# Expert outputs weighted by their gates and added onto x in DRAM by the scatter itself; the first weight chunk loaded in halves

## What is computed

```python
x = x + mix @ w_out                      # "x2" below
xn2 = rmsnorm(x, n2)
# hier_moe: each token goes to 2 of 64 experts, with a gate for each
hdn = silu(xblk @ w1[e]) * (xblk @ w3[e])        # 1024 -> 256
yb = hdn @ w2[e]                                 # 256 -> 1024
y = segment_sum(yb * g_buf[:, None], tok_buf)    # weighted by the gate, summed by token
x = x + y
y_prompt, y_sample = rmsnorm(x, final_norm_g)
```

## Time and profile before

| | us |
|---|---|
| median of 3 runs (lowest, highest) | 1863.19 (1863.05, 1865.97) |
| the profiled execution: its time | 1865.4 |
| the profiled execution: its span | 1863.5 |
| PE busy | 1763.6 (95%) |
| DVE / ACT / POOL busy | 585.1 / 449.3 / 240.2 |

### The profile page before, as it was taken

How to read it: one execution, slowest core, us unless ns; L and a number is a source line. 1 busy time by engine, 2 the same in 40 slices (tenths; PEclk the granted TensorE clock), 3 DMA queues, 4 the chain that set the end, 5 groups by cost and what they waited for, 6 DMA issues and landing times.

```text
span 1863.5 us, 27679 instructions
## 1 busy us (share of the span) xinstructions
PE 1763.6 (95%) x11544; PEld 1477.6 (79%) x11544; DVE 585.1 (31%) x1076; ACT 449.3 (24%) x802; POOL 240.2 (13%) x297
## 2 busy tenths in 40 slices
PE   8999999999999999999999999999899888878885
PEld 8999999999888888899999998887555545544542
DVE  5000102432233323255215337655233111111115
ACT  6221225632222222231222104212111111111113
POOL 0003210000001001000000000000332222222221
PEclk9999999999999999999999999999999999999998
DMA  4222223244435535267616435244799999999997
GB/s 156 94 94 95 70 85 125 95 153 140 125 119 181 165 114 177 99 216 262 226 41 227 140 94 196 92 160 177 318 423 424 425 424 424 424 424 424 424 377 293
DMA packets 159478, 406.34 MB, mean 218 GB/s; under 512 B 20341, under 2 KB 102133, under 8 KB 134778
## 3 DMA queue, kind: packets, MB, share of 16 engines
q1 hardware_dynamic: 137402, 344.22, 49.5%
q0 software_dynamic: 21952, 60.34, 8.3%
HBM read 340.62 MB, written 79.60 MB: 225 GB/s over the span
## 4 chain that ended last, share of the span: by engine, by line
PE 88%; issue 5%; DMA 2%; DVE 2%; ACT 1%; DVEq 0%; SPq 0%; POOLq 0%; POOL 0%; ACTq 0%
PE ps L2006 16%; PE ps L2008 16%; PE ps L2007 16%; PE ps L2311 12%; PE ps L2204 7%; PE ps L2333 6%; PE ps L2298 2%; PE ps L2312 1%; PE ps L2322 1%; PE ps L2095 1%; PE ps L2105 1%; PE ps L2106 1%; PE ps L2019 1%; DMA SG<-feat 1%; PE ps L2372 1%
## 5 line engine op out<-in xcount | busy, mean ns | idle before, releaser
L2006 PE MATMUL ps<-XH,WH 128*128 128x384 f32 (+1 forms) x1152 | 383.1, 333 | 0.0
L2008 PE MATMUL ps<-XH,WL 128*128 128x384 f32 (+1 forms) x1152 | 377.4, 328 | 0.0
L2007 PE MATMUL ps<-XL,WH 128*128 128x384 f32 (+1 forms) x1152 | 377.3, 328 | 0.0
L2311 PE MATMUL ps<-E,yt 128*64 128x256 f32 x1024 | 251.9, 403 | 56.9 <-issue 55.9
L2312 PE MATMUL ps<-E,yt 128*64 128x256 f32 x1024 | 253.0, 404 | 0.0
L2311 PEld LDWEIGHTS ps<-E,yt 128*64 128x64 f32 x1024 | 143.3, 145 | 120.0 <-issue 64.3
L2006 PEld LDWEIGHTS ps<-XH,WH 128*128 128x128 f32 x1152 | 216.4, 188 | 17.0 <-issue 15.1
L2007 PEld LDWEIGHTS ps<-XL,WH 128*128 128x128 f32 x1152 | 216.6, 188 | 0.0
L2008 PEld LDWEIGHTS ps<-XH,WL 128*128 128x128 f32 x1152 | 216.4, 188 | 0.0
L2006 PE MATMUL ps<-WH,XH 128*128 128x256 f32 (+2 forms) x648 | 185.0, 285 | 4.7 <-DVE XL L1447 4.7
L1453 DVE TENSOR_TENSOR WL<-RAW,WH 128x2048 fp32r<-128x2048 f32 (+1 forms) x34 | 78.1, 2298 | 348.1 <-ACT WH L1153 347.9
(11 more groups left out here) (346 smaller groups left out, 2372.4 us busy)
## 6 DMA issues: line engine op xcount, KB each, us to landing
E<-in_exp_w_dram SPq DMA_DIRECT2D x192, 1024.0 KB, 27.7
RAW<-in_w_in_dram SPq DMA_DIRECT2D x29, 1024.0 KB, 7.8
feat<-OF POOLq DMA_DIRECT2D x20, 1088.0 KB, 8.1
SG<-feat SPq DMA_DIRECT2D x24, 544.0 KB, 4.7
tokd<-OT POOLq DMA_DIRECT2D x10, 1024.0 KB, 7.5
cbuf<-feat SPq DMA_DIRECT2D x16, 544.0 KB, 5.4
X<-in_x_prompt_dram SPq DMA_DIRECT2D x16, 512.0 KB, 3.6
VR<-tokd SPq DMA_DIRECT2D x32, 256.0 KB, 2.9
```

What stands on the lines that cost most here:

```text
L2006: pe.matmul(out, hi, mhi, start=start, stop=False)
L2007: pe.matmul(out, hi, mlo, start=False, stop=False)
L2008: return pe.matmul(out, lo, mhi, start=False, stop=stop)
L2311: pe.matmul(ps[0:BR, 2 + b, 0:DE], XT[b][:, turned(k), :], E1[s][:, 1, k, :], start=(k == 0), stop=(k == KD - 1))
```

## The change

1. **The scatter adds.** While the out projection runs, SP also stores each tile of x2 to DRAM (`keep_x2` into `x2d`, 4.5 MB in all). In the experts, ACT's copy from PSUM multiplies each row by its gate (`scale=gw[:, n]`), and POOL's scatter adds the rows onto `x2d` at the rows that were gathered (`tidx`; `yidx` and `ytok` are gone). Two scatters may not be under way at once, since a token stands in two experts, so each scatter waits until the one before it has landed.
2. **Gates earlier.** The gates must be known by slot before the first output leaves PSUM. `gate_differences`, the exponentials and `gate_weights` move ahead of the experts, 18 one-hot matrices are made by DVE after `x_copy` of expert 0, 18 matmuls on PE (`gate_slots`) sum them behind `h_t` of expert 1, and a copy makes `gw`. ACT's first `y_out` waits for it.
3. **Tail.** SP loads the sums, one row a token (0.5 MB a tile), back into `X2`. ACT squares, DVE scales, SP stores. The gate products on DVE and PE and the scaling on ACT and POOL are gone. The root's table is loaded by ACT ahead of the first tile.
4. **First weight chunk in halves.** Chunk 0 comes as two DMAs of half the rows. ACT and DVE split tile 0 of x first, then each half, and PE starts with the first half.

```diff
             def keep_x2(n):
+                sp.wait_ge(x2_ready, n + 1)
+                sp.dma_start(x2d...[n * P:n * P + rows, :], X2[0:rows, n, :]).then_inc(x2_st[0], 16)
...
-                pool.indirect_dma_start(out=ytok[:, :], out_offset=bass.IndirectOffsetOnAxis(ap=column, axis=0),
+                pool.indirect_dma_start(out=x2d[:, :], out_offset=bass.IndirectOffsetOnAxis(ap=column, axis=0),
                                         in_=YS[b][:], in_offset=None,
-                                        bounds_check=4 * NTOK - 1, oob_is_err=False).then_inc(y_st[b], 16)
+                                        bounds_check=2 * NTOK - 1, oob_is_err=False, compute_op=ALU.add).then_inc(y_st[b], 16)
...
             def scatter(st):
                 n, b = st.n, st.b
                 if n == 0:
-                    pool.wait_ge(r_ix, 2)
+                    pool.wait_ge(x2_st[0], x2_st[1] + 16 * NT)
                 pool.wait_ge(y_ready, n + 1)
-                scatter_by(yidx[:, n:n + 1], b)
+                if st.after(1):
+                    pool.wait_ge(y_st[1 - b], 16 * ((n + 1) // 2))
+                scatter_by(tidx[:, n:n + 1], b)
...
             def y_out(st):
                 if st.after(2):
                     act.wait_ge(y_st[b], st.u * 16)
-                act.activation(YS[b][:], ps[:, 5 + b, :], ACT.Copy).then_inc(y_ready, 1)
+                if st.static and n == 0:
+                    act.wait_ge(r_ix, 2)
+                weight = gw[:, n:n + 1] if st.static else gwx[:]
+                act.activation(YS[b][:], ps[:, 5 + b, :], ACT.Copy, scale=weight).then_inc(y_ready, 1)
...
             def load_c(n):
-                sp.dma_start(FY[n][0:rows], ytok.rearrange("(k n h) c -> n k (h c)", k=2, h=2)[n * P:n * P + rows]).then_inc(cy_in[n][0], 16)
+                sp.dma_start(X2[0:rows_of(n), n, :], rows_of_x2(n)).then_inc(cy_in[n][0], 16)
```

More of the change, by code:

```diff
@@ L461, in overflow @@
                 eng.wait_ge(s_over, 10)
[L463 to L467, removed]
+        GATES_AT = 1
         T_COL = [C_V + CW * i for i in range(4)] + [C_R + CW * i for i in range(4)] + [C_VV, C_VV + CW]
@@ L1102, in _ @@
             experts(expert)
+            for b in range(2):
+                pool.wait_ge(y_st[b], 16 * (NE // 2))
             def again(j):
@@ L1113, in again @@
                 wait_alone(pool, y_ready, st.n + 1)
-                scatter_by(yix[:, 0:1], 0)
+                scatter_by(gix[:, 0:1], 0)
                 wait_alone(pool, y_st[0], (j + (1 + NE // 2)) * 16)
             overflow(pool, blocks_over(pool), again)
[L1118 to L1124, removed]
             barrier(pool, 1)
@@ L1808, in index_columns, with gate_differences @@
                 dve.drain()
-                dve.scalar_tensor_tensor(out=tidx[:, c], in0=u, scalar=hv[:], in1=t, op0=ALU.add, op1=ALU.add)
+                dve.tensor_scalar(tidx[:, c], u, hv[:], None, ALU.add)
+            def gate_differences():
+                dve.tensor_tensor(gva[:], lgt[:, :, 0:GROUPS], gtop[:, :, 0:1].to_broadcast([P, NT, GROUPS]), ALU.subtract)
+                dve.tensor_tensor(gd[:], etop[:, :, 1:2], etop[:, :, 0:1], ALU.subtract)
+                dve.drain().then_inc(r_df, 1)
@@ new lines, in gate_weights @@
+            def gate_weights():
+                dve.wait_ge(r_ex, 1)
+                dve.tensor_reduce(gsm[:], gex[:], AX.X, ALU.add)
+                dve.tensor_scalar(gr[:], gd[:], 1.0, None, ALU.add)
+                dve.drain()
+                dve.tensor_tensor(gr[:], gr[:], gsm[:], ALU.mult)
+                dve.drain()
+                dve.reciprocal(gsm[:], gr[:])
+                dve.drain()
+                dve.tensor_copy(gates[:, :, 0:1], gsm[:])
+                dve.tensor_tensor(gates[:, :, 1:2], gsm[:], gd[:], ALU.mult)
+                dve.drain()
+                dve.memset(gates[NDEC:P, NFULL, :], 0.0)
+                dve.drain()
+                dve.scalar_tensor_tensor(out=gow[:], in0=rk[:], scalar=float(BR), in1=gates[:].rearrange("p t k -> p k t"), op0=ALU.is_lt, op1=ALU.mult)
+                dve.drain()
@@ new lines, in gate_one_hot, with gate_one_hots @@
+            def gate_one_hot(i):
+                return AGn[:, i, :] if i < 2 * KD else AGs[:, i - 2 * KD, :]
+            def gate_one_hots():
+                dve.wait_ge(n2_ready, NT + 1)
+                dve.wait_ge(n2_st[0], 16 * (NT // 2 + 1))
+                for i in range(2 * NT):
+                    dve.tensor_scalar(gate_one_hot(i), slf[:].rearrange("p a r -> p (a r)"), row[:, i % 2, i // 2:i // 2 + 1], gow[:, i % 2, i // 2:i // 2 + 1],
+                                      ALU.is_equal, ALU.mult)
+                dve.drain().then_inc(r_ab, 1)
@@ L1897, in over_count @@
                 dve.drain().then_inc(r_ov, 1)
-            def gate_diagonals(n):
-                rows = rows_of(n)
-                i = WEIGHED.index(n)
-                for k in range(2):
-                    dve.tensor_scalar(GD[0:rows, i, k, 0:rows], ident[0:rows, 0:rows], gates[0:rows, n, k:k + 1], None, ALU.mult)
             def x_copy(st):
@@ L2285, in over_slots, with gate_slots @@
             def over_slots(j):
-                pe.wait_ge(r_ab, NT + j + 1)
+                pe.wait_ge(r_ab, NT + 1 + j + 1)
                 for i in range(3 * j, 3 * j + 3):
-                    last = pe.matmul(ps[:, 7, 0:NOVF], A2[:, i % 6, :], B[:, i % 6, :], start=(i == 0), stop=(i == 2 * NT - 1))
+                    last = pe.matmul(ps[:, 7, 0:2 * NOVF], A2[:, i % 6, :], B[:, i % 6, :, :].rearrange("p a n -> p (a n)"), start=(i == 0), stop=(i == 2 * NT - 1))
+                last.then_inc(r_tb, 1)
+            def gate_slots():
+                pe.wait_ge(r_ab, NT + 1)
+                for i in range(2 * NT):
+                    one_hot = AGn[:, i, :] if i < 2 * KD else AGs[:, i - 2 * KD, :]
+                    last = pe.matmul(ps[:, 7, 384:384 + NE], one_hot, oh[:, i % 2, i // 2, :], start=(i == 0), stop=(i == 2 * NT - 1))
                 last.then_inc(r_tb, 1)
```

236 lines of the change are left out of this document (102 added, 134 removed).

## The result

The changed kernel takes 1932.1 us in the median of four runs (1928.0 to 1935.2), the kernel before 1864.0 beside it: a ratio of 1.0363 with a 95% interval of 1.035 to 1.0376. The profiled execution took 1929.5 us, with a span of 1927.7.

A forecast was written before the change was run, and what follows sets the result against it. The expert stage was taken as DMA-bound, 8.08 us an expert; the change would bring 8.45 us cycles. The last landing moves +38.2, the tail -16.0, so 1863.2 + 22.2 gives 1885 us, range 1845 to 1912.

The forecast's parts named there:

- the scatter's chain: Expert stage: each scatter issued only after the last landed; landing 7.6 plus 0.80 makes 8.40 us a cycle.
- the dear add: Rival, expert stage: split packets or successive read and write, landings 8.4 and more, cycle 9.2, median 1927 us; chance 0.18.
- Start: Kernel start: with the first weight chunk in halves, PE's first product comes 2.4 us earlier, at about 13.6.
- Storing x2, gates: Before the experts: last store costs 0.3 us, one-hots fit, gate matmuls take 2.5 us; first scatter at about 1337.0.
- The add's time on the engines: Expert stage: the destination is read too, twice the DMA engine time, 0.33 us more for each expert.
- The landing: Expert stage: an adding scatter lands 7.6 us after issue under load, where a plain one takes 6.8.
- The two are almost equal.: Expert stage: DMA's 8.41 and the chained scatters' 8.40 us nearly coincide, so 8.45 us a cycle was taken.
- The queue runs empty at times ... which pulls the cycle back.: Expert stage: with waits longer than DMA's 8.4 us, the queue sometimes empties and scatters land in 2.34 us, shortening the cycle.
- the prediction's own conversion from profile to median: Whole kernel: the profile's own time lies 1.9 us above its span and 2.2 us above the runs' median.
- Tail: After the last landing: loads and stores of 8.9 MB take 21.0 us of DMA, 23.7 in all, gaining 16.0.
- Neither limit binds: Rival, expert stage: the add costs engines nothing and lands within 7.3 us, cycle 8.08 to 8.12, 1846 us; chance 0.25.
- second price: First sixteen experts: tied to landings they lose their 6.90 us pace, so the stage costs nearly 64 full cycles.

The follow-up runs named there:

- rows4k: Changed kernel with the adding scatter writing whole 4 KB token rows, half as many descriptors, wait kept: 1915.4 us.
- plain_wait: Changed kernel with a plain scatter instead of the adding one, the wait for the landing before kept: 1852.6 us.
- groups: Changed kernel with experts in the order 0, 8, 16, ..., adding scatter kept, wait for the previous landing dropped: 1880.6 us.
- no_w2: Changed kernel, adding scatter and wait kept, with 59 of 64 loads of the third expert matrix left out: 1840.8 us.
- tail_no_norm: Changed kernel without the tail's final normalisation, each tile stored as soon as its load has landed: 1935.2 us.
- plain corners: Changed kernel with a plain scatter: with the wait 1852.6 us; without it, in the expert order 0, 8, 16, ..., 1855.2 us.
- groups_plain: Changed kernel with experts in the order 0, 8, 16, ..., no wait for the previous landing and a plain scatter: 1855.2 us.
- w4k: Changed kernel with each expert weight load cut in two, pieces of 4 KB instead of 8 KB a partition, scatter and wait kept: 1900.8 us.

## Why the prediction was wrong

It said 1885, in a range of 1845 to 1912; it was 1932.1, in the 0.18 that the range left out. The sign was right and the place too, the scatter's chain. What failed was the length of the landing, and the argument that had kept the dear add unlikely. By the prediction's own steps:

**Start.** 13.6 was said, 13.72 it was. Alone it is worth 3.6 us (1.5 to 4.8).

**Storing x2, gates.** The one-hots fit: `hid` of expert 0 starts at 1324.33, before the 1326 that was named as the limit. The gate products are 36 records, not 18, and take 4.2 us instead of 2.5, because each product makes two records: those in the earlier trace rows were counted as one a product. The first scatter came at 1338.0 instead of 1337.0.

**The add's time on the engines.** 0.33 us was said; 25.4 us over 64 experts are 0.40, and the queues' shares give 0.47. Right in kind, a little small: a 4 KB packet took 327 ns adding (`rows4k`) and 159 plain. The Trainium skill (DMA: Bandwidth & Descriptors, "SDMA does more than copy") describes the add as a reduction of two streams, without a price. The doubling that the prediction drew from it agrees in kind with 0.40 to 0.47 us on top of a plain 0.33.

**The landing: the step that failed.** 7.6 us was taken, because a gather, which reads, lands only 0.3 us later than a scatter. It was 8.5. Unloaded, the adding scatter takes 3.7 where the plain one takes 2.34, which is 1.3 us of its own; 0.57 us of that is POOL's longer instruction if it all counts. Weights streaming add 8.5 - 3.7 = 4.8 us to it, and 6.8 - 2.34 = 4.5 to the plain one. So the load's part was known from the rows, and the unloaded part was the unknown to bound. The other term of the chain held: 0.80 us from landing to next scatter was said, 0.85 it was.

The rule of the Trainium skill (DMA: Bandwidth & Descriptors, "Anatomy of one DMA"), 2.0 us plus bytes over 436 GB/s, holds for the plain scatter in an empty queue (2.3 us in `plain_wait`), not for the adding one: with its bytes counted twice it gives an estimate of 2.6 us, and the row says 3.6 to 3.9. Beside streaming weights it holds for neither.

**"The two are almost equal."** With 8.41 by DMA and 8.40 by the chain the sum took 8.45. Apart, the engines' price alone is 25.4 us and the chain on top of it 50.8. The DMA term was about right: in `groups`, where weights bind, the later cycles take 349.6 / 42 = 8.32 us.

```profile
L1090 POOL DMA_INDIRECT x2d<-YS,tidx x43: 1581/1582/1602, 1461.7 to 1811.3; - x43
```

The chain's was not. From the first scatter to the fifty-ninth 530.5 us passed (1338.0 to 1868.5), 9.15 each, where 490.1 were said: +40.4, of the 42.0 us by which the profile ended later than 1885.7. The last five took 27.8 us instead of 32.2, and the last landing 3.6 instead of 2.7.

**"The queue runs empty at times ... which pulls the cycle back."** This was the argument against the dear add, whose number, 1927, is nearly what came (by the prediction's own conversion from profile to median, its 1929 stays 1929), and whose cycle of 9.2 is what came. Of its two conditions, the packets were split, but `rows4k`, which undoes that, shortened the landing by 0.6 us only; whether read and write follow one another, no run shows. Its mark, engines that idle, hardly showed: the share stayed at 0.98 to 1.00, against 1.03 in `groups`, as I read it because a load that has room starts at once, so that every scatter meets weights (no run separates that). And `no_w2` shows how weak the pull is: nearly a third of the weights away, and the landing is still 6.4 us.

**Tail.** 23.7 us was said, 27.8 it was, so the gain was 12 us and not 16. The mechanism, loads and stores on the DMA engines, is what `tail_no_norm` shows; the term was mis-sized mainly because 424 GB/s was taken for all of it. The engines were busy for 23.8 us instead of 21.0, at 311 and 326 GB/s in two stretches, and the rest of the 4.1 us lies in the thinly used ends, with shares of 0.66 and 0.32. For the 1.7 us ahead of the loads and the receipt of 1 the prediction named no row.

**Neither limit binds.** The plain corners, 1852.6 and 1855.2, are what this rival's 1846 stood for. They are later by 6.6 and 9.2 us, of which the tail's term is 4. Its fear that even a plain landing takes the early experts' lead came true, 7.61 us a cycle where 7.6 was said, but it cost nothing: later experts won it back, and `plain_wait` is no slower than `groups_plain`. So the "second price" of the chain, the lost lead, is paid only where the chain stays slower than the weights to the end, as with the add.

The change of +68 us is thus -11.0 for everything but the add, and +79.5 for the add in its chain: about 25 for its own time on engines that were full, about 51 for the wait, and 3 that lie within the spread of the runs.

## What to carry to other kernels

Before work is moved from a tail into a stage bound by DMA, count it in that stage's currency: the change saved 12 us of tail, and its add cost 25 us of engine time before any wait. Where a change chains transfers one behind another, the landing under load is the price. Here the unloaded landing of the new kind plus what the load adds to the old kind, 3.7 + 4.5 = 8.2 us, would have come near the 8.5; if the data allows an order in which neighbours are independent, the chain can be dropped. A DMA share of 1 does not say that bytes bind: look at the GB/s, and at whether the big loads are backlogged or early.

## What was not expected of the hardware

- An adding indirect DMA of 64 token rows keeps POOL 1.58 us instead of 1.01 and lands in 3.6 to 3.9 us instead of 2.3 when the weights are in. With rows of 2 KB it goes out in more packets: 26048 on POOL's queue instead of 21952, with the same bytes. With rows of 4 KB it has 21952 too, and takes the engines as long.
- A share of 0.98 to 1.00 stood beside 370 to 378 GB/s in the changed kernel, and one of 1.03 beside 402 in `groups`, with the same packets on the two large queues. In `w4k` it was 1.03 to 1.04 beside 389 to 399 GB/s, while a landing still released 61 of 64 scatters. The share did not tell the two limits apart.
- Of the 4.8 us that streaming weights add to an adding scatter's landing, about 2.7 pass before its first packet moves, whatever the size of the weights' pieces (`w4k`) or the number of the scatter's packets (`rows4k`).
- The size of other transfers' pieces sets part of a landing: weights in pieces of 4 KB instead of 8 KB made the scatter's landing 7.5 instead of 8.4 us.
